# GpSimd in place of ScalarE scales the dilated-attention maps, between the biases it makes

## What is computed

```python
for window, dilation in DIL_PAIRS:          # (128, 1), (512, 4), (2048, 16)
    sc = q . k[qpos - offs] * scale - slope * offs     # offs = 0, dilation, 2*dilation, ... window
    m, e, l = max(sc), exp(sc - m), sum(e)
o = sum(wts * outs) / sum(wts)              # wts = l * exp(m - max of all m)
```

## Time and profile before

| | |
|---|---|
| median of 3 runs | 334.11 us (333.4 to 334.76) |
| the profiled execution | 334.44 us |
| its span, first to last instruction | 332.6 us |
| PE busy | 296.6 us (89%) |
| DVE busy | 240.2 us (72%) |
| ACT busy | 202.8 us (61%) |
| POOL busy | 12.2 us (4%), 20 instructions |
| DMA | 70.30 MB, mean 211 GB/s |

### The profile page before, as it was taken

The page is one execution under the profiler, slowest core; times in us unless marked ns, Lnnn a source line. Parts: engine busy times, 40 slices in busy tenths (PEclk is TensorE's granted clock), DMA queues, the critical chain, the costliest instruction groups (busy, mean ns, idle before and its releaser), DMA issues.

```text
span 332.6 us, 4776 instructions
## 1 busy us (share of the span) xinstructions
PE 296.6 (89%) x1693; PEld 238.2 (72%) x1693; DVE 240.2 (72%) x487; ACT 202.8 (61%) x406; POOL 12.2 (4%) x20
## 2 busy tenths in 40 slices
PE   2299998999989989797989699999999999988895
PEld 2177776776555768685777478888887799887683
DVE  3899999879783763799878756979773544469533
ACT  4634588555565757998157635576664796897300
POOL 0000000000005440000000000000000000000000
PEclk9999999999999999989999979999999999999999
DMA  7999999563687496386854717578647246100011
GB/s 258 366 415 410 408 405 360 183 235 104 239 310 257 164 367 230 96 291 231 287 167 143 241 67 224 171 299 283 198 163 263 73 145 207 48 17 2 0 63 63
DMA packets 19878, 70.30 MB, mean 211 GB/s; under 512 B 2192, under 2 KB 2576, under 8 KB 19856
## 3 DMA queue, kind: packets, MB, share of 16 engines
q1 hardware_dynamic: 19856, 70.01, 58.6%
HBM read 68.95 MB, written 1.05 MB: 210 GB/s over the span
## 4 chain that ended last, share of the span: by engine, by line
PE 52%; DVE 25%; ACT 12%; DMA 6%; issue 4%; SPq 0%; DVEq 0%; ACTq 0%
PE proj L1049 36%; PE score L1049 8%; DVE w_lo L725 7%; DVE raw L741 6%; DMA raw<-in_w 5%; PE mixed L1049 3%; ACT w_hi L453 2%; PE turned L1094 2%; PE turned L1076 2%; DVE y L918 1%; DVE gt L910 1%; DVE xs L935 1%; DVE hy_lo L925 1%; DVE sq L932 1%; DVE probs L993 1%
## 5 line engine op out<-in xcount | busy, mean ns | idle before, releaser
L725 DVE TENSOR_TENSOR w_lo<-raw,w_hi 128x1024 fp32r<-128x1024 f32 x72 | 87.1, 1220 | 14.9 <-ACT w_hi L453 14.6
L453 ACT ACTIVATE w_hi<-raw 128x1024 fp32r<-128x1024 f32 x72 | 74.9, 1050 | 17.0 <-DMA raw<-in_w 15.4
L1049 PE MATMUL proj<-w_hi,hy_hi 128*128 128x512 f32 x152 | 63.4, 417 | 10.1 <-DVE hy_lo L775 6.0
L1049 PE MATMUL proj<-w_lo,hy_hi 128*128 128x512 f32 x152 | 60.7, 400 | 0.0
L1049 PE MATMUL proj<-w_hi,hy_lo 128*128 128x512 f32 x152 | 60.7, 399 | 0.0
L741 DVE CUSTOM_DVE_ANT_0 raw<-raw,c_rows 128x1024 f32<-128x1024 f32 x48 | 57.8, 1223 | 0.0
L1049 PE MATMUL proj<-hy_hi,w_hi 128*128 128x256 f32 x176 | 53.1, 302 | 0.0
L1049 PE MATMUL proj<-hy_lo,w_hi 128*128 128x256 f32 x176 | 50.4, 287 | 0.0
L1049 PE MATMUL proj<-hy_hi,w_lo 128*128 128x256 f32 x176 | 50.4, 286 | 0.0
L1049 PEld LDWEIGHTS proj<-w_hi,hy_hi 128*128 128x128 f32 x152 | 29.4, 194 | 19.1 <-issue 5.1
L1049 PEld LDWEIGHTS proj<-hy_hi,w_hi 128*128 128x128 f32 x176 | 34.3, 195 | 2.1 <-issue 2.1
(11 more groups left out here) (142 smaller groups left out, 402.6 us busy)
## 6 DMA issues: line engine op xcount, KB each, us to landing
raw<-in_w SPq DMA_DIRECT2D x80, 512.0 KB, 4.6
raw<-in_w_mod SPq DMA_DIRECT2D x48, 512.0 KB, 5.6
xs<-in_x SPq DMA_DIRECT2D x1, 1024.0 KB, 5.1
out_x<-xs SPq DMA_DIRECT2D x4, 256.0 KB, 2.0
cst<-in_constants SPq DMA_DIRECT2D x1, 520.0 KB, 6.4
logits<-in_a_lambda SPq DMA_DIRECT2D x1, 128.0 KB, 11.7
rows<-in_vectors SPq DMA_DIRECT2D x1, 64.0 KB, 1.9
cst<-in_constants SPq DMA_DIRECT2D x1, 64.0 KB, 2.1
```

The lines of the kernel that those rows point to most:

```text
L453: nc.scalar.activation(w_hi[:, slot(n), :, :], raw_tile(("w", n)), ACT.Copy).then_inc(hi_done, 1)
L725: nc.vector.tensor_tensor(w_lo[:, slot(n), :, :], raw_tile(("w", n)), w_hi[:, slot(n), :, :], ALU.subtract).then_inc(lo_done, 1)
L1049: return nc.tensor.matmul(o, a, b, start=start, stop=stop, skip_group_check=True)
```

## The change

GpSimd multiplies the maps of group B by their inverse sums, with TENSOR_SCALAR, in place of ScalarE's activation with a scale. Its program becomes: biases 8 to 12, map 8, bias 13, map 9, bias 14, map 10, bias 15, map 11, and then maps 12 to 15. Each map waits for its `inv_ok` as before, and signals the same `prob_ok`. Nothing else is changed.

```diff
@@ scalar engine
-            def scale_map(j, o):
-                M = 2 * j + o
-                act.wait_ge(inv_ok, M - 7)
-                for tile, cs in enumerate((slice(0, P), slice(P, MAPW))):
-                    i = nc.scalar.activation(probs[:, M % 4, cs], probs[:, M % 4, cs], ACT.Copy,
-                                             scale=stat[:, M % 4, 4 + tile:5 + tile])
-                i.then_inc(prob_ok, 1)
...
-                    for o in range(2):
-                        for j in pairs_at(layer, g, 3 + o):
-                            if group(j) == 1:
-                                scale_map(j, o)
@@ gpsimd engine
+            def scale_map(M):
+                pool.wait_ge(inv_ok, M - 7)
+                for tile, cs in enumerate((slice(0, P), slice(P, MAPW))):
+                    i = nc.gpsimd.tensor_scalar(probs[:, M % 4, cs], probs[:, M % 4, cs], stat[:, M % 4, 4 + tile:5 + tile],
+                                                0.0, ALU.mult, ALU.add)
+                i.then_inc(prob_ok, 1)
             pool.wait_ge(cst_in, 16)
             wait_turned(pool, ("qk", 0, Q2, 1))
             for M in range(8, 16):
...
                 nc.gpsimd.tensor_scalar(b, dist, slope(M // 2, M % 2), 0.0, ALU.mult, ALU.add).then_inc(bias_a, 1)
                 pool.wait_ge(bias_a, M - 7)
                 nc.gpsimd.tensor_tensor(b, b, dilated, ALU.add).then_inc(bias_ok, 1)
+                if M >= 12:
+                    scale_map(M - 4)
+            for M in range(12, 16):
+                scale_map(M)
```

## The result

The changed kernel takes 337.04 us (median of 4 runs, 336.47 to 337.5) against 333.75 us before (4 runs, 333.29 to 334.76). The ratio of the runs is 1.008, with a 95% interval of 1.0051 to 1.0108: slower by 0.5 to 1.1% (the two medians alone lie 1.0% apart). The forecast was 335.5 us with a range of 333.2 to 337.6; the time lies in the range, at its upper end, but the step up is 3.3 us where 1.4 were forecast, more than twice as much.

What follows compares the result with a forecast made beforehand. TensorE was taken to bound the kernel until 127.2 us, VectorE's full queue from 135.47, TensorE from 191.54. Terms 0 + 1.15 + 0.2 = 1.35 us on 334.44 gave 335.8, less 0.33 for the median: 335.5 us, range 333.2 to 337.6.

Steps and rivals of the forecast that it cites:

- ScalarE's relief is worth 0: Term for the eight scaling pairs leaving ScalarE, 6.3 us in all, none on the chain: 0 gained.
- TensorE's waits before maps 13 and 15: Sign in the changed profile: these waits for ScalarE's copy, 1.87 and 1.97 us, would get shorter.
- Where the loss is made: Claim that GpSimd's queue of map 8, bias 13 and map 9 delays TensorE's projection at 119.35 us by 1.15 us.
- 1.15 us: Term for TensorE's projection after map 9's turn starting at 120.5 in place of 119.35 us.
- the first of the five: GpSimd scales map 8: narrow half 114.6 to 114.9, wide half to 115.3 us; VectorE's next product pushed by 0.2 us.
- The pair's own time: GpSimd's narrow and wide halves for one map, taken as 0.30 and 0.40 us; ends 0.50 and 1.46 us.
- Maps 12 to 15: Term for the later maps: 12 and 13 cost nothing, 14 and 15 cost VectorE 0.2 us for both.
- GpSimd starves: Rival: VectorE keeps winning, map 8's wide half waits until 118.4 us; 3.1 us delay, 337.4 us; chance 0.08.
- The clock falls: Rival: TensorE's longer idle gap before map 9's turn halves its clock, costing 1.7 us, 337.2 us; chance 0.27.
- All hidden: Rival: GpSimd's halves slip in without waiting and end at 117.2 us, before map 9's turn; 334.1 us; chance 0.13.
- relief: Rival: ScalarE holds VectorE's stretch, so maps 12 and 13 give back up to 1.6 us; 333.7 or 332.5 us; chance 0.12.
- its own bounds: Limits on the delay at map 9: 0.6 us with cheap pair and payment, about 2.0 with the dear pair.

Runs made afterwards that it cites:

- e4: Kernel before with the scaling of group B left out on every engine, maps unscaled; 334.42 us, ratio 0.9994 to the kernel before.
- e7: Kernel before with VectorE, not ScalarE, scaling group B's maps right behind the reciprocal; 336.6 us, ratio 1.0059 to the kernel before.
- e3: Changed kernel, but GpSimd scales only maps 8 and 9, ScalarE keeps 10 to 15; 336.31 us, ratio 1.009 to the kernel before.
- e2: Changed kernel, but ScalarE keeps maps 8 and 9, GpSimd scales 10 to 15; 334.88 us, ratio 1.0022 to the kernel before.
- e1: Changed kernel, with bias 13 made before maps 8 and 9 are scaled, bias 15 before 10 and 11; 335.44 us, ratio 1.0033 to before.
- e10: Changed kernel, but GpSimd multiplies the maps by a fixed 0.125, not the inverse sums; 336.82 us, ratio 1.0084 to the kernel before.
- e5: Changed kernel plus two VectorE memsets, around the weight split behind the sub-normalisation's product; 336.95 us, ratio 1.0087 to the kernel before.
- e11: Kernel before with VectorE's last gate product of layer 0's four gates given to GpSimd; 334.73 us, ratio 1.0029 to the kernel before.

## Why the prediction was right or wrong

- **What bounds the kernel, and that ScalarE's relief is worth 0: right.** e4 gives 0.9994, and e7 shows VectorE as the bound behind 135 us. TensorE's waits before maps 13 and 15 changed from 1.87 and 1.97 to 1.12 and 3.65 us; both were forecast to be shorter, and the second is longer; neither change shows in VectorE's run, which sets the end.
- **Where the loss is made: right.** It was put at maps 8 and 9, ahead of the projection at 119.35 us, with bias 13 in the queue; e3 has all of the early loss, e2 none, and e1 shows the share of bias 13. It then went through ScalarE's copy to VectorE's queue and to 194.63 us as the text had it.
- **Its size: wrong by more than half.** The term "1.15 us" measured 2.6 (at VectorE's first split), which is beyond the 0.6 to 2.0 us that were given as its bounds. The failed step is the first of the five: "Wide half: 114.9 to 115.3, if it is there before VectorE's 114.94", with the alternative that map 8 comes 0.9 later "and map 9 at the same place within 0.1". It wasn't there before, and then it lost the port once more: ready at 117.56 on the old axis and not at 115.3, or 0.9 us behind that. From then on each step stands later by one to two of VectorE's instructions, and map 9 is ready at 121.59 where 120.1 was forecast. What was assumed from rows with a fixed factor (in at the next gap) doesn't hold for a factor from SBUF. With a fixed factor, e10, the steps came out as written, on the old axis: the first half of bias 13 done at 116.67 (116.65 forecast), the second at 118.33 (118.35), for which VectorE paid 0.52 us (0.55, not the full 0.73), and map 9 ready at 119.94 (120.1).
- **The pair's own time:** 0.70 us taken, 0.83 measured; a small part. But the wide half came 0.11 us behind the start of VectorE's product, where 0.04 us ahead of it was forecast: 0.08 us because the pair began later behind the reciprocals, and 0.07 us because the narrow half took 0.37 and not 0.30. In e10, both shorter and with the product 0.1 us later, it was ahead.
- **Maps 12 to 15: right.** 0.2 us forecast, 0.3 measured: a product pays 0.08 and the low part of the gates, at 150.97 us, lasts 0.87 in place of 0.69.
- **The rivals.** "GpSimd starves" had the mechanism, in a harsher form than was measured (three instructions of VectorE and not two), and the nearest step, 3.3 us up to 337.4; it got 0.08, because one row of an instruction of another form spoke against it. "The clock falls", with 337.2 us, is nearest to the 337.04 by number alone, but it didn't happen in the changed kernel's profile; it did in those of e5 and e10, so part of its chance was deserved. "All hidden" and "relief" are out.
- **The range.** It holds the measured time because it was drawn wide enough for these two slower rivals. For the account that the forecast rests on this is luck: its own bounds end at 2.0 us for the term that measured 2.6.

## What to carry to other kernels

Before work goes to GpSimd, look at what VectorE does in the microseconds in which its result is due. If long instructions with two SBUF operands stand there back to back, a GpSimd instruction that reads SBUF can, as here, wait for the rest of one of them on top of its own time, and for the whole of the next one too if it reads its factor from SBUF; and what is queued ahead on GpSimd can wait in the same way. The same work on maps 10 to 15, mostly where VectorE idled or read PSUM, cost only 0.3 us, so it is the place that decides; and an engine relieved behind another's full queue gave nothing back.

## What was not expected of the hardware

- A GpSimd TENSOR_SCALAR of 128x256 with its factor in SBUF lasts up to 2.09 us (and 2.51 us for map 8) beside VectorE instructions of 1.2 us, the same with a fixed factor at most 1.02 us.
- A memset of 0.17 us between two such VectorE instructions did not let it in.
- A GpSimd instruction with two SBUF operands of 128x512 held VectorE for 1.1 us of its 1.29 (e11) and one of 128x256 for 0.52 us of its 0.73 (e10), where those of 128x256 with one tensor operand cost 0.12 to 0.20 us.
